# Differential attention scores as three zero-padded matmuls, with GpSimd's weight split in four pieces and a new order of the differential groups

## The reference, cut to what matters

```python
def _diff_attend(q, k, v, q_pos, k_pos, lam):
    s = jnp.einsum('bqhd,bkhd->bhqk', q, k, preferred_element_type=jnp.float32) * (DIFF_QK_DIM ** -0.5)
    allowed = (k_pos[None, :] // CHUNK) <= (q_pos[:, None] // CHUNK)
    p = jax.nn.softmax(jnp.where(allowed[None, None], s, -jnp.inf), axis=-1)
    ...
    a = p[:, :, 0] - lam * p[:, :, 1]
    return jnp.einsum('bhqk,bkhe->bqhe', a.astype(v.dtype), v)
```

## Time and profile before

| | |
|---|---|
| median of 3 runs | 1572.53 us (1572.46 to 1573.02) |
| the profiled execution | 1572.31 us, its span 1570.5 us |
| mean granted TensorE clock | 0.977 of full |
| busy: PE / DVE / ACT / POOL | 1491.7 / 664.8 / 640.1 / 608.8 us |
| w_lo on GpSimd, line 1128 | 199 instructions, 470.1 us |
| the chain that ended last | PE 84%, DVE 6%, issue 5%, ACT 2%, POOL 2% |

### The profile page before, as it was taken

The page is one execution under the profiler, slowest core; times in us unless marked ns, Lnnn a source line. Parts: engine busy times, 40 slices in busy tenths (PEclk is TensorE's granted clock), DMA queues, the critical chain, the costliest instruction groups (busy, mean ns, idle before and its releaser), DMA issues.

```text
span 1570.5 us, 29582 instructions
## 1 busy us (share of the span) xinstructions
PE 1491.7 (95%) x10831; PEld 1465.7 (93%) x10831; DVE 664.8 (42%) x1144; ACT 640.1 (41%) x1110; POOL 608.8 (39%) x292
## 2 busy tenths in 40 slices
PE   6788888899999999999998999999999999999996
PEld 5788888899999999999998999999899999999996
DVE  6677767645111111111238888886511111111212
ACT  5566666644222222222235666665432222222121
POOL 3343433333444444433322233222354444443331
PEclk9899989999999999999999999999999999999998
DMA  4212122112222222222232222221222222222222
GB/s 166 66 63 75 63 71 74 59 54 68 83 88 84 80 80 80 77 88 80 79 108 63 77 68 80 83 62 62 68 84 88 82 80 80 80 80 85 83 78 83
DMA packets 41557, 123.76 MB, mean 79 GB/s; under 512 B 4625, under 2 KB 9233, under 8 KB 41505
## 3 DMA queue, kind: packets, MB, share of 16 engines
q1 hardware_dynamic: 41504, 123.06, 23.9%
HBM read 111.21 MB, written 11.83 MB: 78 GB/s over the span
## 4 chain that ended last, share of the span: by engine, by line
PE 84%; DVE 6%; issue 5%; ACT 2%; POOL 2%; DMA 0%; DVEq 0%; SPq 0%; ACTq 0%; POOLq 0%
PE ps L503 72%; PE ops L618 3%; PE tps L575 2%; PE sps L554 2%; DVE acc L1249 1%; POOL w_lo L1128 1%; PE sps L559 1%; POOL qsw L1133 1%; DVE pr L1334 1%; PE ops L608 1%; PE sps L561 1%; PE tps L589 1%; PE sps L563 1%; DVE xT L1258 1%; DVE k L1296 0%
## 5 line engine op out<-in xcount | busy, mean ns | idle before, releaser
L1128 POOL TENSOR_TENSOR w_lo<-w_raw,w_hi 128x1024 fp32r<-128x1024 f32 (+1 forms) x199 | 470.1, 2362 | 822.2 <-ACT w_hi L808 822.2
L503 PE MATMUL ps<-xh,w_hi 128*128 128x288 f32 x2176 | 488.3, 306 | 22.3 <-DVE xl L1526 11.8
L503 PE MATMUL ps<-xl,w_hi 128*128 128x288 f32 x2176 | 472.7, 299 | 0.0
L503 PE MATMUL ps<-xh,w_lo 128*128 128x288 f32 x2176 | 472.3, 299 | 0.0
L808 ACT ACTIVATE w_hi<-w_raw 128x1024 fp32r<-128x1024 f32 (+1 forms) x200 | 208.5, 1043 | 444.6 <-PE ps L503 441.7
L503 PEld LDWEIGHTS ps<-xh,w_hi 128*128 128x128 f32 x2176 | 353.7, 193 | 25.3 <-issue 23.8
L503 PEld LDWEIGHTS ps<-xl,w_hi 128*128 128x128 f32 x2176 | 357.0, 192 | 0.0
L503 PEld LDWEIGHTS ps<-xh,w_lo 128*128 128x128 f32 x2176 | 356.7, 192 | 0.0
L503 PE MATMUL ps<-hl,w_hi 128*128 128x288 f32 x704 | 151.1, 295 | 0.0
L503 PE MATMUL ps<-hh,w_lo 128*128 128x288 f32 x704 | 151.0, 295 | 0.0
L503 PE MATMUL ps<-hh,w_hi 128*128 128x288 f32 x704 | 150.9, 295 | 0.0
(11 more groups left out here) (169 smaller groups left out, 1829.7 us busy)
## 6 DMA issues: line engine op xcount, KB each, us to landing
w_raw<-w_units SPq DMA_DIRECT2D x184, 512.0 KB, 3.3
w_raw<-w_units SPq DMA_DIRECT2D x16, 384.0 KB, 2.9
xT<-x_in SPq DMA_DIRECT2D x8, 288.0 KB, 5.8
dk_out<-kf SPq DMA_DIRECT2D x8, 288.0 KB, 2.1
dv_out<-vf SPq DMA_DIRECT2D x8, 288.0 KB, 4.2
fk_out<-kf SPq DMA_DIRECT2D x8, 288.0 KB, 4.0
fv_out<-vf SPq DMA_DIRECT2D x8, 288.0 KB, 4.1
y_out<-yt SPq DMA_DIRECT2D x8, 288.0 KB, 2.3
```

The lines of the kernel that those rows point to most:

```text
L503: mm = nc.tensor.matmul(out[:, half, :], w[:, k, :], rhs[:, kt, half * HALF:(half + 1) * HALF], start=start and w is w_hi[slot] and rhs is ...
L1128: nc.gpsimd.tensor_tensor(w_lo[slot][:, 0:kts, :], w_raw[slot][:, 0:kts, :], w_hi[slot][:, 0:kts, :].bitcast(F32), ALU.subtract).then_inc( ...
```

## The change

Four things. **Scores:** in the differential layer `q1` now holds the hi part of a map in its own 64 rows and zeros in the other 64 (as `q2` already did for the lo part), and `k1` holds the hi part of both maps in one plane and the lo part in the other, so a score is three matmuls of the full height, `q1`·K_hi, `q1`·K_lo, `q2`·K_hi, and the mask. **Splits:** `k_hi` and `k_lo` become one instruction each over 128 partitions; the two casts of `q_lo` go. Two more memsets at the start clear the halves of `q1`. **Weights:** the lo part is computed in four instructions of 256 numbers per partition (three where a unit has six slices), with one signal after the last. **Order:** new ticks for the differential groups. The forgetting layer keeps its scores and its order.

```diff
-                nc.tensor.matmul(out, q1[:, h, q], k1[par][:, h, k], start=True, stop=False)
-                if L == FOX:
+                if L == DIFF:
+                    for qt, hl in ((q1, 0), (q1, 1), (q2, 0)):
+                        nc.tensor.matmul(out, qt[:, h, q], k1[par][:, hl, k], start=qt is q1 and hl == 0, stop=False)
...
-                else:
-                    nc.tensor.matmul(out, q2[:, h, q], k1[par][:, h, k], start=False, stop=False)
...
+                if L == DIFF:
+                    nc.scalar.activation(k1[par][:, 0, :], kf[:], ACT.Copy).then_inc(kh_done, 1)
...
-                nc.gpsimd.tensor_tensor(w_lo[slot][:, 0:kts, :], w_raw[slot][:, 0:kts, :],
-                                        w_hi[slot][:, 0:kts, :].bitcast(F32), ALU.subtract).then_inc(w_lo_done, 1)
+                for k in range(0, kts, 2):
+                    part = nc.gpsimd.tensor_tensor(w_lo[slot][:, k:k + 2, :], w_raw[slot][:, k:k + 2, :],
+                                                   w_hi[slot][:, k:k + 2, :].bitcast(F32), ALU.subtract)
+                part.then_inc(w_lo_done, 1)
...
+                if L == DIFF:
+                    tt(k1[par][:, 1, :], kf[:], k1[par][:, 0, :].bitcast(F32), ALU.subtract).then_inc(kl_done, 1)
...
-                nc.vector.tensor_copy(q1[64:128, 0, 0:T], q1[0:64, 0, 0:T].bitcast(F32))
-                nc.vector.tensor_copy(q1[0:64, 1, 0:T], q1[64:128, 1, 0:T].bitcast(F32))
+                if L == FOX:
+                    nc.vector.tensor_copy(q1[64:128, 0, 0:T], q1[0:64, 0, 0:T].bitcast(F32))
+                    nc.vector.tensor_copy(q1[0:64, 1, 0:T], q1[64:128, 1, 0:T].bitcast(F32))
...
-    DIFF: dict(S=[4, 4, 14, 20, 28, 36, 45, 46, 59, 60], T=[25, 37, 50, 80, 85], PVS=[39], PVP=[94], VT=0, SS=112),
+    DIFF: dict(S=[5, 5, 11, 21, 23, 35, 36, 49, 60, 61], T=[23, 37, 60, 73, 84], PVS=[64], PVP=[92], VT=7, SS=115),
```

More of the change, by code:

```diff
@@ L71 @@
 ACT_AT = {
-    DIFF: dict(EXP=[4, 8, 14, 20, 30, 37, 49, 49, 58, 64], P=[24, 36, 44, 74, 84], V=11, OS=[77], OSH=[], O=[92],
-               SCALE=109, OH=126, W=[35, 84, 93], SWAP=[42, 67], KH=52, KH2=-1, QH=91),
+    DIFF: dict(EXP=[8, 10, 15, 22, 27, 36, 49, 53, 63, 67], P=[22, 40, 58, 82, 84], V=12, OS=[67], OSH=[], O=[104],
+               SCALE=117, OH=123, W=[30, 82, 89], SWAP=[39, 70], KH=54, KH2=-1, QH=86),
     FOX: dict(EXP=[5, 8, 16, 24, 34, 38, 53, 53, 65, 73], P=[15, 24, 29, 40, 45, 55, 71, 76, 84, 94], V=13, OS=[25, 66],
@@ L76 @@
 DVE_AT = {
-    DIFF: dict(MAX=[8, 11, 15, 18, 32, 34, 43, 55, 58, 68], W=[-1, 12, -1, 30, -1, 37, -1, 58, -1, 76], P=[33, 40, 62, 80,
-               84], OS=[90], OSL=[], OL=[], NORM=119, SPLIT=130, K=36, RK=57, KL=73, Q=69, RQ=93, QL=99, AUG=-1,
-               V=94),
+    DIFF: dict(MAX=[9, 11, 20, 20, 24, 30, 43, 54, 55, 65], W=[-1, 12, -1, 29, -1, 36, -1, 60, -1, 81], P=[33, 46, 78, 83,
+               84], OS=[99], OSL=[], OL=[], NORM=121, SPLIT=126, K=33, RK=54, KL=82, Q=74, RQ=85, QL=96, AUG=-1,
+               V=100),
     FOX: dict(MAX=[1, 9, 11, 12, 27, 32, 43, 47, 59, 62], W=[10, 11, 17, 24, 39, 50, 52, 60, 60, 81], P=[16, 22, 29, 41,
@@ L83 @@
 POOL_AT = {
-    DIFF: dict(OSQ=91, VL=1, SIN=[33, 38], W=[20, 50, 55]),
+    DIFF: dict(OSQ=91, VL=0, SIN=[9, 15], W=[6, 47, 57]),
     FOX: dict(OSQ=-1, VL=12, SIN=[], W=[66, 70, 96])}
-LAST_TICKS = {DIFF: 131, FOX: 102}
+LAST_TICKS = {DIFF: 127, FOX: 102}
 NORM0_AT = 3
@@ L553, in score @@
                         pe.wait_ge(mask_done, 1)
-                nc.tensor.matmul(out, q1[:, h, q], k1[par][:, h, k], start=True, stop=False)
-                if L == FOX:
+                if L == DIFF:
+                    for qt, hl in ((q1, 0), (q1, 1), (q2, 0)):
+                        nc.tensor.matmul(out, qt[:, h, q], k1[par][:, hl, k], start=qt is q1 and hl == 0, stop=False)
+                else:
+                    nc.tensor.matmul(out, q1[:, h, q], k1[par][:, h, k], start=True, stop=False)
                     if jj == 0:
@@ L853, in k_hi @@
                 act.wait_ge(kpast_loaded, val((g + (G * L + 1)) * 16))
-                act.wait_ge(pads_zero, val(4 * (L + 1) + 2))
+                act.wait_ge(pads_zero, val(4 * (L + 2)))
                 if some((g + (G * L - 1)) * 10):
@@ L860, in k_hi @@
                     act.wait_ge(ps_read, val(g * 3 + (N_LAYER * L + 1)))
-                nc.scalar.activation(k1[par][0:64, 0, :], kf[0:64, :], ACT.Copy)
-                nc.scalar.activation(k1[par][64:128, 1, :], kf[64:128, :], ACT.Copy).then_inc(kh_done, 1)
+                if L == DIFF:
+                    nc.scalar.activation(k1[par][:, 0, :], kf[:], ACT.Copy).then_inc(kh_done, 1)
+                else:
+                    nc.scalar.activation(k1[par][0:64, 0, :], kf[0:64, :], ACT.Copy)
+                    nc.scalar.activation(k1[par][64:128, 1, :], kf[64:128, :], ACT.Copy).then_inc(kh_done, 1)
             def k_hi_again(g, par):
@@ L1294, in k_lo @@
                 dve.wait_ge(kh_done, val(g + (G * L + 1)))
-                tt(k1[par][64:128, 0, :], kf[0:64, :], k1[par][0:64, 0, :].bitcast(F32), ALU.subtract)
-                tt(k1[par][0:64, 1, :], kf[64:128, :], k1[par][64:128, 1, :].bitcast(F32), ALU.subtract
-                   ).then_inc(kl_done, 1)
+                if L == DIFF:
+                    tt(k1[par][:, 1, :], kf[:], k1[par][:, 0, :].bitcast(F32), ALU.subtract).then_inc(kl_done, 1)
+                else:
+                    tt(k1[par][64:128, 0, :], kf[0:64, :], k1[par][0:64, 0, :].bitcast(F32), ALU.subtract)
+                    tt(k1[par][0:64, 1, :], kf[64:128, :], k1[par][64:128, 1, :].bitcast(F32), ALU.subtract
+                       ).then_inc(kl_done, 1)
             def q_lo(L, g):
@@ L1495, in clear_pads @@
                 if L == DIFF:
-                    nc.vector.memset(q2[64:128, 0, 0:T].bitcast(F32), 0.0).then_inc(pads_zero, 1)
-                    nc.vector.memset(q2[0:64, 1, 0:T].bitcast(F32), 0.0).then_inc(pads_zero, 1)
+                    for q in (q1, q2):
+                        nc.vector.memset(q[64:128, 0, 0:T].bitcast(F32), 0.0).then_inc(pads_zero, 1)
+                        nc.vector.memset(q[0:64, 1, 0:T].bitcast(F32), 0.0).then_inc(pads_zero, 1)
                 nc.vector.memset(kf[:, T:TQ], 0.0).then_inc(pads_zero, 1)
```

## The result

The changed kernel takes **1522.23 us** (median of 4 runs, 1521.43 to 1522.99) against 1572.78 us before: ratio 0.9677, interval 0.9661 to 0.9694. The profiled execution took 1521.43 us, its span is 1519.6 us, its mean granted clock 0.991 (before 0.977).

What follows compares the result with a forecast made beforehand. Layer 0's groups were taken to lose 58.7 us: 35.9 of PE waiting and 22.8 of lowered clock. From 1572.3, less 58.7, plus 12.8 for the third matmul and 8 of residue: 1534 us, range 1524 to 1562.

Steps and rivals of the forecast that it cites:

- The third matmul: New PE work in layer 0's scores, with nothing to hide it once PE is full: 1.60 us a group, 12.8 us for eight.
- the residue: Layer 0's groups: 0.7 us for the late second chain (exponential, weighing, transposes), 0.3 for the first score; 8 us over eight.
- Rival D: Layer 0's groups: everything closes, with no waiting left over; 1526 us, chance 0.08.
- stages taken at nothing: Start and ahead of SwiGLU: turns between VectorE and GpSimd only spread the same delay; no gain, -2 to +2 us.
- Q's way and PE's side: From VectorE taking Q: lo part ready after 10.1 us (before 14.14), PE asks for the first score after 10.7 (before 14.24).
- The casts: Two copies on Q's way ahead of its lo part; without them that way is 1.55 us shorter.
- K's joined splits: Saves about an instruction each on ScalarE and VectorE, off the path, as both had idle time; counted at nothing.
- The order: Layer 0's groups: one more slice (0.79 us) and the sample's product (some 0.7) before the first score, V's transposes (0.5) out.
- The pieces: GpSimd's w_lo in four pieces of 0.70 us: VectorE waits for one piece, not up to 2.35 us; w_lo comes 0.38 later.
- A: Layer 0's first score still waits, 1.3 us a group, the clock dropping after every second wait; 1556 us, chance 0.21.
- B: GpSimd runs its pieces as one block, so the first score's wait and clock loss stay; 1570 us, no change, chance 0.05.
- C: The head's square on GpSimd comes late, PE waits around its sum `SS`, 3.3 us a group plus clock; 1575 us, chance 0.10.

## Why the prediction was right and wrong

Direction and mechanism were right, the size was 12 us too small, and the range's low end, 1524, was 1.8 us too high. Point by point:

- **What bounds the kernel: right.** Waits and clock of layer 0's groups came to 58.7 us; less 12.8 for the third matmul that is 45.9, and from the second group's first slice to SwiGLU the traces differ by 46.7.
- **The third matmul: right**, 12.8 forecast, 12.9 measured for a fourth. By the spacings in the Trainium skill (TensorE: Matmul & The Clock Gate, Back-to-back issue gap) it would be 8.6, an estimate on a straight line between them; the measurement decides for the rows.
- **The step that failed: the residue, 8 us.** It was to cover a second chain that comes late and a first score whose bounds touch. It measured 0: PE is busy for 213.66 of 213.66 us. I had the reason for the last transpose's wait before me (a weighing held up by GpSimd) and had moved that weighing away, and still kept 0.7 us a group for it. Rival D, no residue, with a chance of 0.08, was the true one for the groups; at 1526 us it misses the rest by the next step.
- **The other step: stages taken at nothing.** Outside layer 0's groups I forecast no gain, and the stages there gave 4.2 us together, 3.0 of them at the start, up to the second group's first slice (its first score comes 4.7 us earlier, 44.55 for 49.20). I argued that turns only spread the same delay where VectorE is full. The runs with one part show the first score at 46.14 with the split alone, 46.98 with the scores alone, 49.17 with the order alone. The first wait of both SwiGLU blocks fell from 2.19 to 1.28 and 1.27 us, inside my -2 to +2. The clock that the shorter wait keeps up in the first block, 1.6 us, I had no term for.
- **Q's way and PE's side: right in sum, too cautious in what I made of them.** 9.6 us measured, 10.1 (9.4 to 11.5) forecast; PE's side 196.96 - 186.46 = 10.5, forecast 10.7.
- **The casts: their size was off alone.** 1.55 us were 2.9 in the run of the scores alone, since the lo part behind them left the next weight's span.
- **K's joined splits at nothing: right in the old order, by the 0.07 us that let the weighing pass, wrong in the new.** Undone in the whole change they cost 6.9 us, 4.4 of them at the last transpose. I had called ScalarE and VectorE idle enough there; both come to the split of the transposes within 0.07 us of each other, and too late.
- **The order: wrong alone.** I counted one slice and the sample's product as gained time for Q. Alone it makes Q's way 1.3 us longer; only with pieces does the rotation get through (0.89 us for 2.81).
- **The pieces: right.** Four take 2.82 us where I gave 2.79, so a whole weight comes 0.43 us later for 0.38; the two lo instructions take 1.82 us where I gave 1.5 to 2.2.
- **Rivals A, B, C fell.** No first score waits, the scores alone and the split alone each all but end its clock loss (1.00 and 0.99), and `SS` is in no row of PE's waits, so C's place shows nothing.

For the range: D was no extreme, since it is what follows when each wait that the argument closes is closed. A low end 2 us below it allowed the border stages 2 us where they gave 4.2.

## What to carry to other kernels

Where two engines exclude each other, ask of each short instruction on the waited path which long one it starts behind; cut the long one so far that its pieces are short beside the slack, and no further, since each piece has a fixed cost (here 0.14 us) and each border may give a turn away. An instruction that leaves a path can save more than its own time when the next ones fall out of such a span, so shift the rows behind it and look where they land. And when a stall's cause is removed, give its rest a place and a price, or take it at zero.

## What the runs showed of the hardware

- An add of 64 columns by VectorE, 0.23 us alone, took 2.28 us when a GpSimd weight had begun 0.42 us earlier; a difference of 0.07 us at the start decided whether a weighing took 0.35 or 1.50 us.
- A GpSimd subtraction of 1024 numbers a partition took 2.39, 2.53, 2.82 and 3.39 us in one, two, four and eight instructions: 0.14 us for each further one. Beside a busy VectorE eight took up to 5.04 us.
- PE's clock: waits of 2.6 us and of 3.35 to 3.64 us (order alone, 0.94 over 200 us) went with a lower granted clock; waits of up to 1.6 us, one a group, did not (scores and order, 1.00). Of the waits of 2.19 us ahead of the two SwiGLU blocks before, one was followed by 0.86 over 12 us and one by 1.00, so the length of a wait alone does not tell.
